# Memory's keys and values computed among the items of the differential attention, and rows and keys turned inside the second output projection

## What is computed

```python
# mixer: differential attention (4 heads, 2 score maps of 64 dims each), beside a gated linear attention
dq = _rmsnorm(dq, da_qn); dk = _rmsnorm(dk, da_kn)
def probs(qb, kk):
    sc = jnp.einsum('bhqd,bhkd->bhqk', qb, kk).astype(jnp.float32) * scale
    return jax.nn.softmax(jnp.where(mask, sc, -jnp.inf), axis=-1)
p = probs(qb1, k1) - lam * probs(qb2, k2)          # blocks of 128 queries, mask by chunks of 64
da = _rmsnorm(einsum(p, v), da_on) * (1.0 - lam_init)
h = h + concatenate([da_out, gla_out]) @ w_o        # the second output projection

# cross attention of the 1024 rows to a memory of 256 rows
u = _rmsnorm(h, norm_g);  mn = _rmsnorm(mem, norm_m)
q = _rmsnorm((u @ w_q).reshape(b, s, 4, 256), qn)
kv = mn @ w_kv                                      # 256 x 1024 times 1024 x 2048
k = _rmsnorm(kv[..., :d].reshape(b, m, 4, 256), kn);  v = kv[..., d:]
...
```

## Time and profile before

| | us |
|---|---|
| median of 3 runs | 3038.17 (3028.83 to 3039.26) |
| the profiled execution, its own time | 3037.15 |
| its span in the trace | 3035.2 |
| PE busy | 2859.2 (94%) |
| attention items, first score to last value | 1764.85 to 1911 |
| second output projection, to its last matmul | 1911 to 2017.04 |
| keys and values, rows turned | 2017.04 to 2092.46 |
| first two query groups | 2092.46 to 2105.20 |

### The profile page before, as it was taken

How to read it: one execution, slowest core, us unless ns; L and a number is a source line. 1 busy time by engine, 2 the same in 40 slices (tenths; PEclk the granted TensorE clock), 3 DMA queues, 4 the chain that set the end, 5 groups by cost and what they waited for, 6 DMA issues and landing times. The chain is left out here.

```text
span 3035.2 us, 32823 instructions
## 1 busy us (share of the span) xinstructions
PE 2859.2 (94%) x13162; PEld 2136.7 (70%) x13162; DVE 1814.4 (60%) x2676; ACT 1174.6 (39%) x1788; POOL 401.7 (13%) x242
## 2 busy tenths in 40 slices
PE   8999898999999999999999988899999799999998
PEld 3445576777888888885457855765777678887777
DVE  5785556567444455454356347422223589999998
ACT  3101644323221111134334345233332367777776
POOL 1022400004000000012000000000000027333332
PEclk9999999999999999999999999899999899999999
DMA  9320100011111111113001010130010689999996
GB/s 327 111 70 28 53 1 1 29 56 65 47 49 49 42 56 54 44 42 140 1 1 42 15 70 1 56 139 28 1 36 30 238 330 369 388 383 382 380 376 259
DMA packets 120448, 363.13 MB, mean 120 GB/s; under 512 B 14474, under 2 KB 48552, under 8 KB 95712
## 3 DMA queue, kind: packets, MB, share of 16 engines
q1 hardware_dynamic: 103760, 330.19, 29.6%
q0 software_dynamic: 16528, 30.76, 2.8%
HBM read 356.69 MB, written 29.38 MB: 127 GB/s over the span
## 5 line engine op out<-in xcount | busy, mean ns | idle before, releaser
L182 PE MATMUL PS<-BIG 128*128 128x512 f32 (+10 forms) x2448 | 646.6, 437 | 41.8 <-ACT BIG L2390 15.2
L182 PEld LDWEIGHTS PS<-BIG 128*128 128x128 f32 (+4 forms) x2448 | 336.2, 187 | 289.4 <-issue 236.2
L3066 DVE TENSOR_TENSOR ML<-MR,MH 128x2048 fp32r<-128x2048 f32 x144 | 329.9, 2303 | 28.3 <-ACT MH L3061 27.9
L182 PE MATMUL PS<-MH,MX 128*128 128x512 f32 x1024 | 322.4, 396 | 12.5 <-DVE ML L3066 10.5
L3061 ACT CAST MH<-MR 128x2048 fp32r<-128x2048 f32 x144 | 275.4, 1914 | 94.4 <-DMA MR<-in_w_e_up 46.3
L182 PEld LDWEIGHTS PS<-MH,MX 128*128 128x128 f32 x1024 | 190.0, 189 | 57.2 <-DVE ML L3066 17.7
L182 PE MATMUL PS<-FWH,FHH 128*128 128x512 f32 x512 | 200.0, 391 | 4.2 <-DVE XR L1635 2.0
L182 PE MATMUL PS<-FXH,FWH 128*128 128x512 f32 x512 | 200.2, 391 | 1.1 <-DVE FWL L1487 1.1
L182 PE MATMUL PS<-ML,MX 128*128 128x512 f32 x512 | 200.5, 392 | 0.0
L182 PE MATMUL PS<-FXH,FWL 128*128 128x512 f32 x512 | 199.9, 390 | 0.0
L182 PE MATMUL PS<-FXL,FWH 128*128 128x512 f32 x512 | 199.8, 390 | 0.0
(11 more groups left out here) (484 smaller groups left out, 5372.0 us busy)
## 6 DMA issues: line engine op xcount, KB each, us to landing
MR<-in_w_e_gate SPq DMA_DIRECT2D x50, 1024.0 KB, 19.0
MR<-in_w_e_up SPq DMA_DIRECT2D x48, 1024.0 KB, 21.1
MR<-in_w_e_down SPq DMA_DIRECT2D x46, 1024.0 KB, 19.5
FWR<-in_w_ff SPq DMA_DIRECT2D x32, 1024.0 KB
XR<-in_w_e_down SPq DMA_DIRECT2D x18, 1024.0 KB, 18.4
BC<-in_w_ada SPq DMA_DIRECT2D x32, 512.0 KB, 3.6
XR<-in_w_e_up SPq DMA_DIRECT2D x16, 1024.0 KB, 21.0
XR<-in_w_e_gate SPq DMA_DIRECT2D x14, 1024.0 KB, 19.5
```

Of the source, the lines that this page charges most:

```text
L182: ins = pe.matmul(o, l, r, start=(start and n == 0), stop=(stop and n == len(pairs) - 1), skip_group_check=True)
L3066: dve.tensor_tensor(cut_at(ML, i), raw(i), cut_at(MH, i).bitcast(F32), ALU.subtract).then_inc(e.w_lo.up(), 1)
```

## The change

The memory's rows are loaded, normed and turned during the last third of stage 1. The 64 matmuls become 128 of 128x256 (`pe_ckv(n)`), and pass n of the attention issues `CK_PARTS[n]` of them behind its values: 5 in passes 0 to 11, 4, 6, 5, 5 in 12 to 15, then 0, 4, 3, 3, 3, 3 three times over. The keys are squared by ACT in passes 16 to 19 (`act_ck_squares`), scaled by POOL behind pass 22 (`pool_ck_norm`), and turned behind rows 0 to 3 of the second output projection; the rows are turned behind its rows 5 and 6 (`wo2_pe_after`). The weights come in eight loads of 1 MB. So that this has room: the mask matmuls read fp32r copies (`DMASK`); the result of an item lies in bank 6 alone, and ACT scales it out (`da_ev`) and squares it from SBUF (both lines are new for ACT, the scaling was DVE's); `x_back0` is loaded behind the last key matmul; both halves of `w_cq_2` lie where the cut high parts need the projection's end (`wo2_mm[32]`). The buffers of the cross attention move from `BC` to slot 10, and three small POOL loads for the router wait for somewhat later points of it.

```diff
+        def pool_mem():
+            G.wait_ge(*mt_ok[8])
+            G.wait_ge(*d_mm[48])
+            gps.tensor_copy(MEMT[1], MEMT[0]).then_inc(mt_copy.up(), 1)
...
         def sp_da():
             for i in range(2, 6):
                 sp_dfetch(i)
+            S.wait_ge(*dw_lo[5])
+            sp.dma_start(MEM, X["mem_2"][0].rearrange("(t p) d -> p t d", p=128)).then_inc(mem_in.up(), 16)
+            S.wait_ge(*dw_lo[6])
+            sp_ckv(0)
+            S.wait_ge(*mt_tr[4])
+            sp_ckv(1)
...
                 if k_ - 2 in DA_DONE[:16]:
                     pe_da_turn(DA_DONE.index(k_ - 2))
+                if 39 <= k_ < 43:
+                    pe_mem_turn(k_ - 39)
...
+        CK_PARTS = (5,) * 12 + (4, 6, 5, 5, 0) + (4, 3, 3, 3, 3, 0) * 3
...
+        def pe_ckv(n):
+
+            for x in range(CK_FROM[n], CK_FROM[n + 1]):
+                k, at = divmod(x, 16)
+                n_, t = divmod(k, 2)
+                kk, hh = divmod(at, 2)
+                if at == 0:
+                    before = [j for j in range(k) if CK_BANK[j] == CK_BANK[k]]
+                    P.wait_ge(*(ck_ev[before[-1] + 1] if before else bank[CK_BANK[k]]))
+                    P.wait_ge(*(mt_ok[8] if k < 4 else mt_copy[1]))
+                P.wait_ge(*ckv_in[2 * n_ + kk // 4][1])
+                ins = mm(PS[:, CK_BANK[k], 256 * hh:256 * hh + 256],
+                         [(MEMT[k // 4][:, kk, 128 * t:128 * t + 128], CKW[2 * n_ + kk // 4][:, kk % 4, 256 * hh:256 * hh + 256])],
+                         start=(at == 0), stop=(at == 15))
...
+        def pool_ck_norm():
+            G.wait_ge(*ck_rs[1])
             for t in range(2):
...
+                for dc in range(2):
+                    o = CK4[:, dc, :, 128 * t:128 * t + 128]
+                    gps.tensor_tensor(o, o, b4(css8[:, 4 * t:4 * t + 4], 128), ALU.mult).then_inc(ck_n.up(), 1)
+
+        def sp_ckv_rest():
+            S.wait_ge(*d_mm[48])
+            for i in range(2, 5):
+                sp_ckv(i)
+            sp_wo2_first()
+            S.wait_ge(*ck_mm[2])
+            for i in range(5, 7):
+                sp_ckv(i)
+            S.wait_ge(*ck_mm[4])
+            sp_ckv(7)
 
         def sp_da_back0():
-            S.wait_ge(*d_mm[48])
+            S.wait_ge(*ck_mm[8])
...
                     for m in range(2):
-                        mm(sflat(n, m)[:, nk - 128:nk], [(C("ident"), C("chm"))], start=False).then_inc(da_s.up(), 1)
+                        mm(sflat(n, m)[:, nk - 128:nk], [(EYE_R, CHM_R)], start=False).then_inc(da_s.up(), 1)
...
-                    P.wait_ge(*(da_ev[k - 1] if k >= 2 else bank[6 + k]))
-                    mm(PS[:, 6 + k % 2, 0:128], [(PT2[k % 2][:, 128 * j:128 * j + 128], DV[:, j, 128 * h:128 * h + 128])
+                    P.wait_ge(*(da_ev[k] if k else bank[6]))
+                    mm(PS[:, 6, 0:128], [(PT2[k % 2][:, 128 * j:128 * j + 128], DV[:, j, 128 * h:128 * h + 128])
                                                  for j in range(i + 1)]).then_inc(da_o.up(), 1)
+                pe_ckv(n)
+            pe_ckv(NI + 2)
...
+                if 2 <= n <= NI + 1:
+                    k = n - 2
+                    h, i = ITEMS[k]
+                    do = DO[:, i, 128 * h:128 * h + 128]
+                    A.wait_ge(*da_o[k + 1])
+                    A.wait_ge(*da_r[k + 1])
+                    act.activation(do, PS[:, 6, 0:128], ACT.Copy, scale=da_sm(k, 0)[3]).then_inc(da_ev.up(), 1)
+                    A.wait_ge(*da_ev[k + 1])
+                    A.wait_ge(*da_sq.last)
+                    act.activation(SQD, do, ACT.Square, accum_out=dos[:, i, h:h + 1]).then_inc(da_sq.up(), 1)
+                act_ckv(n - 1)
+                if 16 <= n < 20:
+                    act_ck_squares(2 * n - 32, 2 * n - 30)
...
-                if n >= 3:
-                    k = n - 3
-                    h, i = ITEMS[k]
-                    V.wait_ge(*da_sq[k + 1])
-                    dve.tensor_scalar(DO[:, i, 128 * h:128 * h + 128], PS[:, 6 + k % 2, 0:128], da_sm(k, 0)[3], None,
-                                      ALU.mult).then_inc(da_ev.up(), 1)
...
                     V.wait_ge(*da_e[2 * n + 2])
-                    V.wait_ge(*da_sq[max(n - 3, 0)])
+                    V.wait_ge(*da_ev[max(n - 3, 0)])
...
+        def wo2_pe_after(t):
+            if t < 4:
+                pe_ck_turn(t)
+            if 5 <= t < 7:
+                for m in range(4 * t - 20, 4 * t - 16):
+                    pe_ux(m)
...
         def sp_cross():
+            S.wait_ge(*wo2_wok[4])
+            sp.dma_start(*CQW[0]).then_inc(cq_in[0].up(), 16)
             S.wait_ge(*wo2_mm[32])
...
+            sp.dma_start(*CQW[1]).then_inc(cq_in[1].up(), 16)
...
         def act_cw(i):
             A.wait_ge(*cq_in[i // 2][1])
...
+            A.wait_ge(*wo2_mm[32])
```

More of the change, by code:

```diff
@@ L158, in program, with layout @@
         ctx.callback(lambda: area[0].close())
-        def layout(*parts, rows=None):
+        def layout(*parts, rows=None, tail=()):
             area[0].close()
@@ new lines, in act_mem, with dve_mem @@
+        def act_mem():
+            A.wait_ge(*mem_in[1])
+            for t in range(2):
+                A.wait_ge(*mem_sq.last)
+                act.activation(SQC, MEM[:, t, :], ACT.Square, accum_out=mss[:, t:t + 1]).then_inc(mem_sq.up(), 1)
+            A.wait_ge(*mem_sq[2])
+            act.activation(mss, mss, ACT.Sqrt, scale=1.0 / 1024, bias=epsc[:, 1:2]).then_inc(mem_std.up(), 1)
+        def dve_mem():
+            V.wait_ge(*mem_std[1])
+            dve.reciprocal(mss, mss).then_inc(vs.up(), 1)
+            V.wait_ge(*vs.last)
+            for t in range(2):
+                dve.tensor_scalar(MEM[:, t, :], MEM[:, t, :], mss[:, t:t + 1], None, ALU.mult).then_inc(mem_ok.up(), 1)
@@ new lines, in pe_mem_turn, with act_mem_turn @@
+        def pe_mem_turn(p):
+            P.wait_ge(*mem_ok[2])
+            P.wait_ge(*(mt_ok[2 * p - 2] if p >= 2 else v_go[8]))
+            for c in (2 * p, 2 * p + 1):
+                for t in range(2):
+                    ins = tr(PS[:, 6 + p % 2, 256 * (c % 2) + 128 * t:256 * (c % 2) + 128 * t + 128],
+                             MEM[:, t, 128 * c:128 * c + 128])
+            ins.then_inc(mt_tr.up(), 1)
+        def act_mem_turn(p):
+            A.wait_ge(*mt_tr[p + 1])
+            A.wait_ge(*v_go[8])
+            for c in (2 * p, 2 * p + 1):
+                act.activation(MEMT[0][:, c, :], PS[:, 6 + p % 2, 256 * (c % 2):256 * (c % 2) + 256], ACT.Copy,
+                               scale=cols["nmem"][:, c:c + 1]).then_inc(mt_ok.up(), 1)
@@ L2199, in act_da @@
                     act.activation(gss, gss, ACT.Sqrt).then_inc(gstd_ok.up(), 1)
+                    act_mem()
+                if q == 20:
+                    for p in range(4):
+                        act_mem_turn(p)
                 A.wait_ge(*d_mm[DA_DONE[q] + 1])
@@ new lines, in program @@
+        CK_FROM = (0,) + tuple(itertools.accumulate(CK_PARTS))
+        CK_LAST = [next(n for n in range(len(CK_PARTS)) if CK_FROM[n + 1] >= 16 * k + 16) for k in range(8)]
+        CK_BANK = (7, 5, 7, 5, 7, 7, 7, 7)
+        assert CK_FROM[-1] == 128
+        def pe_ckv(n):
[11 more added lines that the diff above has]
+                         start=(at == 0), stop=(at == 15))
+                if at == 15:
+                    ins.then_inc(ck_mm.up(), 1)
@@ new lines, in act_ck_squares, with act_ck_std @@
+        def act_ck_squares(a, b):
+            A.wait_ge(*ck_ev[4])
+            for k in range(a, b):
+                t, h = divmod(k, 4)
+                A.wait_ge(*ck_sq.last)
+                act.activation(CSN[:, 0:256].rearrange("p (d n) -> p d n", d=2), CK4[:, :, h, 128 * t:128 * t + 128], ACT.Square,
+                               accum_out=css8[:, k:k + 1]).then_inc(ck_sq.up(), 1)
+        def act_ck_std():
+            A.wait_ge(*ck_sq[8])
+            act.activation(css8, css8, ACT.Sqrt, scale=1.0 / 256, bias=epsc[:, 1:2]).then_inc(ck_std.up(), 1)
@@ L2411, in act_da_att @@
             act_da_std(16, 32)
+            act_ckv(NI + 2)
         def dve_da_inverse(a, b):
@@ L2551, in program @@
-        CQW = [kmajor(6 + n, X["w_cq_2"][0][:, 512 * n:512 * n + 512]) for n in range(2)]
-        CXH, CXL, CWL, CWH = (x[:, :] for x in layout(
-            ("CXH", SL, F32R), ("CXL", SL, F32R), ("CPAD", 2 * SL, F32), ("CWL", 2 * SL, F32R),
-            ("CWH", 2 * SL, F32R)) if "PAD" not in x.name)
-        CXH3, CXL3 = (x.rearrange("p (c n) -> p c n", c=8) for x in (CXH, CXL))
-        css = st("css", 4)
-        KTM2 = [bc(1)[:, 0:512], bc(1)[:, 512:1024]]
+            if t < 4:
+                act_ck_turn(t)
@@ new lines, in wo2_act_after @@
+            if 5 <= t < 7:
+                for m in range(4 * t - 20, 4 * t - 16):
+                    act_ux(m)
+        def wo2_pe_after(t):
+            if t < 4:
+                pe_ck_turn(t)
+            if 5 <= t < 7:
+                for m in range(4 * t - 20, 4 * t - 16):
```

(16 more changed lines are left out.)

285 lines of the change are left out of this document (108 added, 177 removed).

## The result

The changed kernel takes **2988.88 us** (median of 4 runs, 2987.43 to 2991.70) against 3038.72 us (4 runs, 3028.83 to 3041.79): ratio 0.9848, 95% interval 0.9834 to 0.9863, 1.5% faster. The forecast was 2990 us, range 2974 to 3008. Its profiled execution took 2987.43 us with a span of 2985.3.

A forecast was written before the change was run, and what follows sets the result against it. PE, busy 94% of the span, was taken as the bound. Behind the projection -68.4, projection +5.3, stage 1 +1.8, attention +14.5 sum to -46.8 us: from 3037.15 to 2990 us, range 2974 to 3008.

The forecast's parts named there:

- Behind the projection: From the second output projection's last matmul to the first 48 query matmuls' end: 19.8 us in place of 88.2, -68.4 us.
- Items 16 to the last values: Late attention: 45 pieces mostly fill PE's waits, some waits stay; 94.9 us in place of 96.5, -1.6 us.
- The pieces cost a quarter of themselves: Whole attention: grows by 14.5 us, though 128 pieces at 0.44 us are 56.3 us of PE work.
- POOL: Attention: POOL's four products about pass 22 and its copy at the start hold up DVE; 1.5 us taken.
- three signs of being wrong: Attention: a piece's weights not landed, PE waiting for the single result bank (`da_ev`), or a clock that drops; no size given.
- the narrow mask saves nothing: Attention's mask matmuls: fp32r at 128 columns gains nothing, 9.6 us lost, 3000 us; chance 0.10.
- slower: Attention's pieces: weight load, matmul and drain go strictly in turn, 1.07 us a piece, 3071 us; chance 0.02.
- all pieces add: Attention: every piece adds in full and none fills a wait, 43.8 us in place of 14.5, 3020 us; chance 0.02.
- the pieces do not fit: Items 16 to 31: 45 pieces add in full, 108.6 us in place of 94.9, 3004 us; chance 0.12.
- The turns hold the projection's end: Second output projection: the turns delay its end by twice 3.3 us, 2997 us; chance 0.04.
- POOL holds DVE: Attention: POOL's products and copy block DVE instructions with two SBUF inputs, +6.5 us, 2997 us; chance 0.08.
- The waits fill better: Attention: no loss in passes 16, 22, 28 and at POOL, mask at 0.12: -6.9 - 3.2, 2980 us; chance 0.10.

The follow-up runs named there:

- Experiment 6: Changed kernel with the rows' eight turns moved from inside the second output projection to behind its last matmul; one run 2984.32 us, against 2988.88.
- experiments 7 and 8: Changed kernel with query weights' first casts and cuts ahead of row 7's norm, 2982.76 us; separately, with pieces respread over passes 16 to 31, 2988.16 us.
- experiment 5: Changed kernel with two more 0.35 us DVE instructions in every attention item, on a scratch area; 2993.34 us.
- experiment 2: Changed kernel with only 16 of the 128 pieces computed (wrong sums): 2968.64 us; the same with the mask in plain float32: 2968.30 us.
- experiment 4: Changed kernel with eight 128x2048 POOL products ahead of POOL's copy: 2989.01 us; the same with 16 pieces and plain float32 mask: 2977.30 us.
- experiment 1: Changed kernel with the mask matmuls in plain float32 again; 2991.66 us.
- experiment 3: Changed kernel with 64 pieces of 128x512 in place of 128 of 128x256, half the weight loads; 2984.29 us.
- cuts first: Changed kernel with first two query-weight casts and cuts ahead of row 7's norm, second half loaded in two pieces; 2982.76 us, ratio to before 0.9815.
- pieces spread: Changed kernel with pieces in every pass 16 to 31, none behind the last values, ACT's result copies at the start of a pass; 2988.16 us.
- both: Changed kernel with early query-weight casts and cuts and with the pieces respread; 2983.10 us, against 2987.91 for the changed kernel on the same chip.

## Why the prediction was right

It was right in the time and in the place of the time. Over the four stretches it was 3.2 us too high, by three terms of one sign that were each a little large. That the median still lies within 1.1 us of the forecast is in part luck: the last stretch, which nothing touches, alone varies by 9 us between traces.

- **Behind the projection** (-68.4, measured -69.1). The first query matmul came 6.58 us behind the last of the projection, by norm, cast and cut as worked out (6.4). The mis-sized term is the clock: 13 intervals at the lower level were taken from the earlier trace rows as 2.5 us, six were seen in this trace (6 to 14 in the others), so the 48 matmuls took 12.52 us and not 13.4. The 2 MB load landed after 7.7 us (8.7 were taken) and was not waited for by PE.
- **Projection** (+5.3, measured +4.35). No turn was late. Experiment 6 gives 0.42 us a group, 5.1 for twelve; the rest is that the projection starts at the full clock in this trace, 0.47 for its first matmul where it had 0.78, and its first 12 matmuls take 4.20 us and not 4.96. Other traces of the same instructions start at the lower one (experiments 7 and 8), so this part is no gain of the change.
- **Ahead of the attention** (+1.8, measured +1.89). The four groups of turns are there, in full.
- **Items 0 to 15** (64.3 us, measured 63.8, PE never idle). The sum by PE's work alone was the right kind of sum, and experiment 5 shows it directly: 11 us more on DVE cost nothing. Mask pair 0.28 (forecast 0.25), five pieces 2.32 us, 0.45 each (forecast 0.44).
- **Items 16 to the last values** (94.9, measured 94.4). Right sum. But that here the way over DVE and ACT is the bound and PE has room, as I held up to experiment 5, was only half true: both are nearly full. The scores waited for exponentials in four places, 4.3 us in all, where 3 were forecast, and the last turns 1.43 us for their difference (1.5). The last pieces and ACT's copy cost 0.8 us, not 1.4. In all, the attention grew by 12.85 us and not by 14.5.
- **"The pieces cost a quarter of themselves"** was the weak sentence. It held for the net of pieces, mask and freed DVE. By themselves the pieces cost 27 of 49 us (experiment 2), three quarters of their length early and three tenths late.
- **POOL** (1.5 us, seen 0.4). Only one difference met a product:

```profile
1864.06 1.02 DVE L2593 SCALAR_TENSOR_TENSOR XR<-BIG,ST 128x768 f32<-128x768 f32 x1
...
1868.83 1.42 DVE L2593 SCALAR_TENSOR_TENSOR XR<-BIG,ST 128x768 f32<-128x768 f32 x1
```

```profile
1865.38 4.04 POOL L2452 TENSOR_TENSOR BC<-BC,ST 128x512 f32<-128x512 f32 x4 [98.36 <-DVE ST L2445]
```

  The four products took 1.01 us each (1.26 were taken) and met one difference, which lost 0.4 us; the others fell beside two maxima, which kept their 1.82 us. The copy ran from 1765.13 to 1767.02, ahead of the first difference (1768.27). The mechanism of the earlier trace rows is real (experiment 4), its place here was harmless. The reason given, that PE has slack at the start, was wrong: PE has none there, DVE has.

None of the three signs of being wrong showed: between 1765.7 and 1925 PE waited for no weights and not for the one result bank, and the granted clock was 1.00.

Of the rivals, "the narrow mask saves nothing" fell by experiment 1, "slower" by experiment 3, "all pieces add" and "the pieces do not fit" by the late distance: 81.31 us with them, 81.29 before (though early three quarters of each piece did add). "The turns hold the projection's end" fell by the trace: PE's one wait in the projection is 4.42 us, and it was 4.43 before. "POOL holds DVE" is a true mechanism at a harmless place. "The waits fill better" came true by 1.7 us of its 10; its sum was loose besides, since 6.9 us took in more than the passes and POOL that it names (4.5), and the mask from 0.25 to 0.12 is 4.2 us and not 3.2.

## What to carry to other kernels

Before pricing filler work, say for each stretch which engine's own work adds up to its length: where PE's does, more filler or a longer mask counts in full and a held DVE next to nothing (1.1 us for 9.5); where PE waits, a third or less of the filler counted here. Read small edits by distances between landmarks that lie close around them: the early and late ones repeated to 0.01 us where whole times scattered by 6. A distance from the program's start takes in the scatter of all that lies ahead.

## What was not expected of the hardware

- The number of query matmuls at the lower clock did not follow the idle time ahead of them: 6, 7 or 14 intervals behind 6.59 us (ten traces), 12 and 11 behind 4.46, 11 behind 4.98. That alone makes whole times scatter by 1.6 us (8 x 0.2), more than an edit of a small wait brings. What sets it stays open.
- The clock at the start of the projection differs too: behind 2.45 us of idle time its first matmul took 0.47 us in the changed kernel and 0.78 in "cuts first", behind 2.67 us 0.77 in "pieces spread" and 0.47 in "both".
- In the attention the clock fell to 0.50 for some 17 us after an idle time of 1.32 us and light work, and not after 0.83; the kernel before kept 1.00 there, and later even behind 1.50 us. With all pieces it never fell. That the pieces hold the clock up is likely by this, but only one kernel with few pieces and the short mask shows the fall.
- One DVE instruction of 0.35 us took up to 2.09 us beside 3.69 us products on POOL, six times its length, and eight products cost the early items 1.1 or 10.1 us by what else bound them, the second with a fall of PE's clock in it.
